# Banded attention on one core: the softmax division of each pair's first head moves from DVE to POOL, and POOL's other work is laid out anew

## What is computed

```python
def one_block(args):  # 128 queries of one block
    qn, kn, vn, valid_n = args
    s_win = einsum('bqhgd,bkhd->bhgqk', qn, kn) * scale        # own block and its neighbours
    s_win = where(valid_n, s_win, -inf)
    s_ctx = einsum('bqhgd,bchd->bhgqc', qn, k_ctx) * scale      # 256 context keys
    s_sink = broadcast_to(sink_l, s_win.shape[:-1] + (1,))
    p = softmax(concatenate([s_win, s_ctx, s_sink], -1))
    return einsum(p[..., :nw], vn) + einsum(p[..., nw:nw + n_ctx], v_ctx)

def mlstm_out(h, oa):                     # the other mixer, gated
    h = rms_norm(h.transpose(0, 2, 1, 3), a_norm_g)
    return h.reshape(...) * sigmoid(oa)
y = concatenate([mlstm_out(ha, oa), ob], -1) @ w_out
```

## Time and profile before

| | us |
|---|---|
| median of 3 runs | 2442.12 (2442.07 to 2444.85) |
| the profiled execution, device time | 2440.61 |
| its span, first to last instruction | 2438.8 |
| PE busy | 2314.1 (95%) |
| DVE busy | 1143.0 (47%) |
| POOL busy | 1060.4 (43%) |
| ACT busy | 805.5 (33%) |
| mean granted clock of PE | 0.976 of full speed |

### The profile page before, as it was taken

How to read it: one execution, slowest core, us unless ns; L and a number is a source line. 1 busy time by engine, 2 the same in 40 slices (tenths; PEclk the granted TensorE clock), 3 DMA queues, 4 the chain that set the end, 5 groups by cost and what they waited for, 6 DMA issues and landing times. The chain is left out here.

```text
span 2438.8 us, 35010 instructions
## 1 busy us (share of the span) xinstructions
PE 2314.1 (95%) x14335; PEld 1909.8 (78%) x14335; DVE 1143.0 (47%) x1870; ACT 805.5 (33%) x1394; POOL 1060.4 (43%) x719
## 2 busy tenths in 40 slices
PE   6999979999997999989989999999999899999998
PEld 5876757778775789856778888888887687788887
DVE  4647368756635660668254141423348652511111
ACT  4334353332326312356141121112144363322221
POOL 3436335555554122325355352434443024745653
PEclk8999989999998999989999999999999999999999
DMA  8335235535442111114111232322112002233321
GB/s 268 106 104 174 87 105 182 167 121 165 156 160 92 41 52 54 34 53 156 53 50 55 69 113 78 101 88 70 52 45 78 26 1 70 89 102 104 102 82 41
DMA packets 223924, 228.24 MB, mean 94 GB/s; under 512 B 7375, under 2 KB 221347, under 8 KB 223779
## 3 DMA queue, kind: packets, MB, share of 16 engines
q1 hardware_dynamic: 223443, 226.09, 28.8%
q10 hardware_dynamic: 336, 0.11, 0.0%
HBM read 224.08 MB, written 2.10 MB: 93 GB/s over the span
## 5 line engine op out<-in xcount | busy, mean ns | idle before, releaser
L1422 POOL TENSOR_TENSOR w_lo<-ring,w_hi 128x1024 fp32r<-128x1024 f32 x124 | 303.3, 2449 | 312.3 <-ACT w_hi L1416 312.3
L2366 DVE SCALAR_TENSOR_TENSOR xT<-ps,mods,xT 128x512 f32<-128x512 f32 (+1 forms) x160 | 108.3, 683 | 544.2 <-PE ps L1484 508.5
L1416 ACT ACTIVATE w_hi<-ring 128x1024 fp32r<-128x1024 f32 x124 | 130.7, 1057 | 501.6 <-PE ps L1484 501.6
L1482 PE MATMUL ps<-hidden_hi,w_hi 128*128 128x512 f32 (+1 forms) x768 | 272.3, 354 | 0.0
L1483 PE MATMUL ps<-hidden_lo,w_hi 128*128 128x512 f32 (+1 forms) x768 | 272.0, 354 | 0.0
L1484 PE MATMUL ps<-hidden_hi,w_lo 128*128 128x512 f32 (+1 forms) x768 | 271.6, 354 | 0.0
L2657 DVE SCALAR_TENSOR_TENSOR ffn_sums<-ps,cols,ffn_sums 128x441 f32<-128x441 f32 (+2 forms) x352 | 214.9, 685 | 106.1 <-ACT ffn_sums L2576 106.1
L1482 PE MATMUL ps<-h_hi,w_hi 128*128 128x512 f32 (+1 forms) x720 | 255.3, 355 | 1.7 <-POOL w_lo L1422 1.6
L1483 PE MATMUL ps<-h_lo,w_hi 128*128 128x512 f32 (+1 forms) x720 | 255.1, 354 | 0.0
L1484 PE MATMUL ps<-h_hi,w_lo 128*128 128x512 f32 (+1 forms) x720 | 254.6, 354 | 0.0
L2599 POOL TENSOR_TENSOR ffn_w_lo<-ring,ffn_w_hi 128x1024 fp32r<-128x1024 f32 (+2 forms) x76 | 162.2, 2136 | 205.3 <-ACT ffn_w_hi L2549 205.3
(11 more groups left out here) (471 smaller groups left out, 5169.7 us busy)
## 6 DMA issues: line engine op xcount, KB each, us to landing
ring<-in_mlp_w SPq DMA_DIRECT2D x64, 1024.0 KB, 5.3
ring<-in_ada_w SPq DMA_DIRECT2D x48, 1024.0 KB, 5.3
ring<-in_w_ada SPq DMA_DIRECT2D x24, 1024.0 KB, 5.3
ring<-in_ffn_w_up SPq DMA_DIRECT2D x22, 1024.0 KB, 5.2
ring<-in_ab_w_in SPq DMA_DIRECT2D x11, 1024.0 KB, 5.3
ring<-in_ffn_w_down SPq DMA_DIRECT2D x12, 768.0 KB, 4.6
ring<-in_w_in SPq DMA_DIRECT2D x8, 1024.0 KB, 8.5
ring<-in_c_w_in SPq DMA_DIRECT2D x6, 1024.0 KB, 5.1
```

The lines of the kernel that those rows point to most:

```text
L1416: act.activation(w_hi[m][:, 0:x["kt"], :], ring[:, x["n"] % NS, 0:x["kt"], m * P:(m + 1) * P], ACT.Copy).then_inc(SW["w_hi"].sem, 1)
L1422: pool.tensor_tensor(w_lo[m][:, 0:x["kt"], :], ring[:, x["n"] % NS, 0:x["kt"], m * P:(m + 1) * P], w_hi[m][:, 0:x["kt"], :].bitcast(F32), ...
L1482: pe.matmul(o, w_hi[m][:, k, :], h, start=(k == 0), stop=False)
L2366: return nc.vector.scalar_tensor_tensor(x, bank, column_of(gates, t * 2 + 2 * gate + r), x, ALU.mult, ALU.add)
```

## The change

Four edits, all in this stage:

- In `norm` on DVE the reciprocal is still done for both heads, but the multiplication only for head 1. POOL gets a `norm` of its own for head 0, which waits for "den" and signals "normed"; `turn` waits for "normed" ahead of head 0 and for "norm" ahead of head 1.
- In POOL's loop `norm(p)` comes first in iteration p, and `out_split` is done for pair p-1 behind it.
- The six scalings come two at a time behind norm(0), norm(1) and norm(2).
- The four gatings move from pairs 11, 12, 13, 14 to 11, 13, 15, 17, and stand behind that pair's norm.

```diff
@@ band_attention, POOL
-                    mix.scaled(pool)
+                    def norm(p):
+                        width = len(blocks(pairs[p][1])[0]) * CH
+                        b = 2 * (p % 3)
+                        wait(pool, "den", 2 * p + 1)
+                        sig(pool.tensor_scalar(sc[:, p % 3, 0, 1:1 + width], sc[:, p % 3, 0, 1:1 + width],
+                                               dens[:, b:b + 1], None, ALU.mult), "normed")
+
                     for p in range(n_p):
+                        norm(p)
+                        if p == 0:
+                            mix.first(pool)
+                        if 2 * p < NCH:
+                            mix.scaled(pool, 2 * p)
+                            mix.scaled(pool, 2 * p + 1)
                         if p in mix.side_at:
                             gated_side(pool, mix.side_at.index(p))
-                        out_split(pool, p)
+                        if p:
+                            out_split(pool, p - 1)
                         if p == 19:
                             made.weights_low(pool)
+                    out_split(pool, n_p - 1)
@@ band_attention, PE, turn(p)
-                            wait(pe, "norm", 2 * p + e + 1)
+                            wait(pe, ("normed", "norm")[e], p + 1)
@@ band_attention, DVE, norm(p)
                             sig(dve.reciprocal(dens[:, b:b + 1], dens[:, b:b + 1]), "den")
+                            if e == 0:
+                                continue
                             wait(dve, "den", 2 * p + e + 1)
@@ MixerNorm
-            turn_at, side_at = [3, 4, 5, 6, 9, 10], [11, 12, 13, 14]
+            turn_at, side_at = [3, 4, 5, 6, 9, 10], [11, 13, 15, 17]
...
-            def scaled(self, pool):
+            def first(self, pool):
                 self.wait(pool, "rd", 1)
-                for c in range(NCH):
-                    self.sig(pool.tensor_tensor(self.src[:, c, :, :], h_tok[:, c, :, :],
-                                                ssq[:, c, :].unsqueeze(2).to_broadcast([P, 4, P]), ALU.mult), "scaled")
+
+            def scaled(self, pool, c):
+                self.sig(pool.tensor_tensor(self.src[:, c, :, :], h_tok[:, c, :, :],
+                                            ssq[:, c, :].unsqueeze(2).to_broadcast([P, 4, P]), ALU.mult), "scaled")
```

More of the change, by code:

```diff
@@ L3046, in band_attention @@
             edges = []
-            R = named("edge", "qk", "top", "exp", "den", "norm", "turned", "turned_a", "turned_v", "pv", "pv_out")
+            R = named("edge", "qk", "top", "exp", "den", "norm", "normed", "turned", "turned_a", "turned_v", "pv", "pv_out")
             sig = lambda ins, n: ins.then_inc(R[n].sem, 1)
@@ L3249, in band_attention @@
             for n, v in (("edge", len(edges)), ("qk", n_p), ("top", 2 * n_p), ("exp", 2 * n_p), ("den", 2 * n_p),
-                         ("norm", 2 * n_p), ("turned", 2 * n_p), ("turned_a", n_p), ("turned_v", n_p), ("pv", n_p),
+                         ("norm", n_p), ("normed", n_p), ("turned", 2 * n_p), ("turned_a", n_p), ("turned_v", n_p), ("pv", n_p),
                          ("pv_out", n_p)):
```

## The result

The changed kernel takes 2484.13 us (median of 4 runs, 2482.19 to 2486.37) beside 2442.10 us before: the ratio is 1.0163, with a 95% interval of 1.015 to 1.0175, so it is 42 us slower. The forecast had the sign (slower, at 0.87) and less than half of the size: +18.6 us, 2460.7, and a range that ended at 2474.

A forecast was written before the change was run, and what follows sets the result against it. PE was taken to bound nearly all of the banded attention stage. Ring waits 7.5, gatings 6.3, and L689 with its tail 10.8, less 6.0 of DVE relief, gave +18.6 us: 2442.1 to 2460.7 us, range 2450 to 2474.

The forecast's parts named there:

- What bounds the kernel, and what relief is worth: Banded attention stage: PE bounds nearly everything; lighter DVE saves 2.3 us at transposes and 3.7 before L866, together 6.0.
- The new ring: POOL's norm(p+1) stands behind out_split(p-1), which needs values(p-1), so PE's turns wait: 7.5 us in sum.
- the tail behind L689: Turns after the weights' low halves on POOL: turn 21 +1.5, turn 22 +1.0, turn 23 +1.9 us.
- The gatings and L689: POOL's long work ahead of norms: gatings add 6.3 us; weights' low halves, with the turns after them, 10.8 us.
- POOL's multiplication: Price of the division on POOL, taken from its one-input cast: 0.71, 0.61 and 0.39 us for 640, 512, 256 columns.
- the forecast's own sign of being wrong: The prediction would be wrong if, among other signs, POOL's new multiplication line averaged over 1 us.
- Clock: PE's low-clock loss of some 1.7 us before L866 should recur after the idle time before turn 20: 0.
- The two-input rate: Rival: POOL multiplies at its two-input price, gated turns gain 11 us together: +29.6, 2472 us; chance 0.14.
- The port: Rival: DVE's and POOL's multiplications block one another at the shared port, 2.3 us of relief lost: +20.9, 2463; chance 0.15.
- POOL catches up: Rival: POOL has unseen idle time for gatings and L689, leaving the ring alone: +7.4 us, 2449.5; chance 0.10.
- DVE was the bound: Rival: norm(p+1) on POOL is ready before values(p-1) end, so no turn waits: -7.7 us, 2434; chance 0.05.

The follow-up runs named there:

- the run with the copy: The changed kernel with POOL's multiplication replaced by a plain copy of the same columns, first head's division left out: ratio 1.0054 to the kernel before, median 2459.27 us.
- The run with the order alone: The changed kernel with only POOL's new order kept and both heads multiplied on DVE again: ratio 0.9985 to the kernel before, 2441.07 us; run again, 0.9992.
- the run with the division ahead: The changed kernel with POOL's division of pair p+1 written ahead of out_split(p-1) and of the gating: ratio 1.0049 to the kernel before, 2457.38 us.
- the mended one: The changed kernel with POOL's division ahead of out_split(p-1) in two-input form, gatings at 10, 13, 15, 21, L689 at p = 20: ratio 1.0024, 2449.57 us.
- the run with the two-input multiplication: The changed kernel with POOL's division written as a two-input multiplication, second input each partition's number repeated: ratio 1.0102 to the kernel before, 2471.4 us.

## Why the prediction was right in sign and wrong in size

- **What bounds the kernel, and what relief is worth.** Right. The changed kernel shows no turn waiting for DVE and no wait ahead of L866: the 6.0 us were had, and were small.
- **The new ring.** Right. Waits appear at the turns named and none at turns 4, 5, 6, 10, 11 and 17; one of 0.67 us at turn 1, which I had not named, comes with the higher price. Where POOL's price is the forecast's, in the run with the copy, they are 20.6 us against 24.6, and turns 7, 8, 13, 19 and 20 come within 0.12 us. Turns 2, 3, 9 and 15 were over-sized by some 0.3 us each, and the tail behind L689 by 1.4 us in all: turns 21, 22 and 23 wait 1.19, 0.15 and 1.61 us, against 1.5, 1.0 and 1.9. The 0.20 us from POOL's signal to PE was read a little low: the rows that it names give 0.26, and so does turn 8 of the changed kernel.
- **The gatings and L689.** Right as terms of the ring (3.41 us against 3.3 at turn 14, 6.47 against 6.4 at turn 20). The run with the order alone shows that they are nothing without it. I forecast 0.4 us at turn 12 where the copy has none and the changed kernel, with its price, 1.50.
- **POOL's multiplication.** This is the step that failed. I took the cast as nearest row, and as far end the two-input operation, and excluded anything beyond for no reason that a row gave: TENSOR_SCALAR on POOL had no row at all. It took 1.95, 1.60 and 0.94 us, 1.49 on average, which is the forecast's own sign of being wrong (over 1 us). Going from the copy to it moves the ratio from 1.0054 to 1.0163, about 27 us, beside a miss of 23 us; by the medians the copy came out some 5 us under my sum. By the profiled executions the stage grows by 22.4 us from the copy to it, 15.4 of them waits for POOL. The page of the Trainium skill (GPSIMD Engine Reference, 3.1 Elementwise) whose best case of 1.8 cycles would give 0.96 us for 640 columns, an estimate, leaned the right way against the cast but is half of the measured 1.95 us; the measurement decides.
- **Clock.** Forecast as 0, one spell for another. Failed as well, and most of it hangs on the price: in the run with the copy PE's work takes 102.0 us of busy time against 99.1 before, in the changed kernel 109.1. So some 2.9 of the 10.0 us come at the forecast's own price, and 7.2 with the real one. Gaps of 2.3 to 2.5 us at turns 2, 13 and 19, forecast as 1.1 to 1.6 us, are there followed by transposes at 1.2 GHz. At turn 8 a gap of 2.71 us is not.
- **The sum, redone.** With the prices of undisturbed divisions (1.88, 1.56 and 0.92 us) the ring's terms grow by 7 x 1.17, 6 x 0.95 and 3 x 0.53 us, in all 15.5, to 40.1 us of waits; 36.0 are measured. Turns 14, 15 and 22 fall short the most, by 3.4 us together; PE's own work ahead of them was slower and covered part of the ring, which no run separates. Idle time of PE grew by 29.9 us (36.0 less the 6.0 of relief), and 10.0 us more are PE's lower clock: 39.9 us in the stage, where the forecast had 18.6. The 21.3 us between them are 11.4 of waits and 10.0 of clock, so the clock is nearly half of the miss.
- **The rivals.** The two-input rate (0.14) was nearest in its mechanism, and still too cheap. The port did not decide in this kernel; once the ring is cut and POOL has the two-input form it draws out DVE's multiplications. That POOL catches up, or that DVE was the bound, is out.

## What to carry to other kernels

Before work moves to another engine, write down what stands ahead of it in that engine's queue and who produces it: a division of some 0.5 us on an engine where nothing slow stood ahead of it became the last link of a ring through the split of the previous result, and most of what the division cost there was paid again at each of some 16 turns. If the trace has no row for an operation on an engine, its price has no upper end from neighbours; leave the range open above, or find the form that has a row (here the broadcast two-input multiplication, a third cheaper). Long work in an in-order queue is free only where nobody waits behind it within its length.

## What the runs showed of the hardware

- On POOL a TENSOR_SCALAR multiplication of float32 costs 1.95 us for 640 columns, and the same multiplication as a TENSOR_TENSOR with a repeated second input 1.28 us; a copy costs 0.74 us. The Trainium skill (GPSIMD Engine Reference, 4.1 Engine selection) calls one-input operations on this engine roughly line rate. The copy agrees, with 0.9 ns more for each column from 256 to 640; the TENSOR_SCALAR with one input and a constant, 1.84 us for 640 columns and 2.5 ns a column, does not, and the measurement decides.
- Which engine comes first went with the form of POOL's instruction, where both multiply at one moment. With the TENSOR_SCALAR form both begin within 0.01 us, DVE runs at its full rate and POOL's takes 2.22 us in place of 1.89, longer by 0.33 us; with the two-input form POOL keeps its 1.25 us and DVE's 0.55 us becomes 1.59. First the run with the division ahead, then the mended one:

```profile
1103.00 0.55 DVE L3202 TENSOR_SCALAR big<-big,small 128x640 f32<-128x640 f32 x1
1103.01 2.22 POOL L3082 TENSOR_SCALAR big<-big,small 128x640 f32<-128x640 f32 x1 [2.40 <-DVE small L3198]
```

```profile
1100.90 1.25 POOL L3082 TENSOR_TENSOR big<-big,small 128x640 f32<-128x640 f32 x1 [3.01 <-DVE small L3198]
1100.92 1.59 DVE L3202 TENSOR_SCALAR big<-big,small 128x640 f32<-128x640 f32 x1
```

The Trainium skill (SBUF — State Buffer, Who interferes with whom) has it that whoever issues first holds the pair for the whole instruction and the other fully blocks. The second pair of rows agrees: DVE ends 0.36 us behind POOL. The first does only in part, as POOL loses 0.33 us to a DVE instruction of 0.55. And POOL's TENSOR_SCALAR does not keep DVE out for its whole length. In the changed kernel this multiplication of DVE begins 0.77 us behind POOL's of 1114.44, takes 0.49 us, as one that meets nothing does, and ends 0.63 us before it:

```profile
1115.21 0.49 DVE L3200 TENSOR_SCALAR big<-big,small 128x512 f32<-128x512 f32 x1
```

Behind POOL's two-input form, begun 0.79 us earlier, the same multiplication takes 0.75 us and ends 0.28 us behind it (the run with the two-input multiplication). For the TENSOR_SCALAR the measurement decides, and not the Trainium skill. When it lets DVE through, and why POOL comes second with the one form and first with the other, is open.
